# Memory attention beside four projection chunks instead of eight, and four seven-product projection units instead of two

## The reference

```python
h = _rms_norm(x, attn_norm_g[l])
proj = h @ w_in[l]          # 2048 x 13312
da_q, da_k, da_v, r_q, r_k, r_v, r_g, m_q, gates = _split_cols(proj, IN_SIZES)
o_da = _diff_attention(da_q, da_k, da_v, ...)
o_ret = _retention(r_q, r_k, r_v, r_g, ...)
o_mem = _memory_attention(m_q, mem, mem_norm_g[l], w_mem_kv[l], ...)
```

## Time and profile before

| | |
|---|---|
| median of three runs | 1628.24 us |
| profiled execution, first to last instruction | 1625.4 us (2.8 us less than that median; a time of its own for this execution, with launch and end, is not shown) |
| PE busy | 1618.2 us (100%) |
| VectorE busy | 1271.1 us (78%) |
| ScalarE busy | 908.2 us (56%) |
| granted TensorE clock | 1.00 over the whole span |

### The profile page before, as it was taken

How to read it: one execution, slowest core, us unless ns; L and a number is a source line. 1 busy time by engine, 2 the same in 40 slices (tenths; PEclk the granted TensorE clock), 3 DMA queues, 4 the chain that set the end, 5 groups by cost and what they waited for, 6 DMA issues and landing times.

```text
span 1625.4 us, 20227 instructions
## 1 busy us (share of the span) xinstructions
PE 1618.2 (100%) x7373; PEld 1339.3 (82%) x7373; DVE 1271.1 (78%) x1325; ACT 908.2 (56%) x989; POOL 80.6 (5%) x73
## 2 busy tenths in 40 slices
PE   9999999999999999999999999999999999999999
PEld 7888888888888888888888888888888888888887
DVE  5565545589777777777975589999999999999995
ACT  6654454555555554445554465656655665656653
POOL 0000000000011100000000000100100100100101
PEclk9999999999999999999999999999999999999999
DMA  9876555556554555566675756868868868868866
GB/s 339 278 214 194 157 180 175 174 179 220 179 166 162 164 172 168 174 188 199 202 245 182 249 166 207 252 211 248 246 212 250 249 208 249 244 220 240 253 211 178
DMA packets 178007, 341.35 MB, mean 210 GB/s; under 512 B 11793, under 2 KB 16401, under 8 KB 177169
## 3 DMA queue, kind: packets, MB, share of 16 engines
q1 hardware_dynamic: 167056, 319.45, 60.4%
q0 software_dynamic: 10880, 20.97, 7.1%
HBM read 317.31 MB, written 2.10 MB: 197 GB/s over the span
## 4 chain that ended last, share of the span: by engine, by line
PE 90%; issue 6%; DVE 1%; DMA 1%; POOL 1%; ACT 1%; SPq 0%; DVEq 0%; ACTq 0%; POOLq 0%
PE acc L1582 43%; PE at L1664 9%; PE at L1666 9%; PE at L1665 9%; PE acc L1666 5%; PE acc L1664 5%; PE acc L1665 5%; PE at L1582 3%; PE at L1604 2%; POOL rstd L480 1%; PE at L1642 0%; PE at L1657 0%; DMA raw<-in_w_mem_kv 0%; DMA raw<-in_w_in 0%; DVE w_lo L929 0%
## 5 line engine op out<-in xcount | busy, mean ns | idle before, releaser
L929 DVE TENSOR_TENSOR w_lo<-raw,w_hi 128x1024 fp32r<-128x1024 f32 x319 | 386.6, 1222 | 239.6 <-ACT w_hi L507 235.4
L507 ACT ACTIVATE w_hi<-raw 128x1024 fp32r<-128x1024 f32 x319 | 337.1, 1060 | 360.9 <-PE acc L1582 300.3
L1582 PE MATMUL acc<-w_hi,hT_hi 128*128 128x512 f32 x752 | 297.6, 396 | 0.0
L1582 PE MATMUL acc<-w_hi,hT_lo 128*128 128x512 f32 x752 | 293.1, 390 | 0.0
L1582 PE MATMUL acc<-w_lo,hT_hi 128*128 128x512 f32 x752 | 293.0, 390 | 0.0
L857 ACT ACTIVATE f_hi<-sum 128x2048 fp32r<-128x2048 f32 x60 | 115.3, 1922 | 121.2 <-DVE sum L1461 118.0
L1582 PEld LDWEIGHTS acc<-w_hi,hT_hi 128*128 128x128 f32 x752 | 141.2, 188 | 30.9 <-issue 1.3
L1582 PEld LDWEIGHTS acc<-w_hi,hT_lo 128*128 128x128 f32 x752 | 141.2, 188 | 29.7
L1582 PEld LDWEIGHTS acc<-w_lo,hT_hi 128*128 128x128 f32 x752 | 141.3, 188 | 28.4
L1582 PE MATMUL acc<-w_hi,oT_hi 128*128 128x512 f32 x384 | 151.2, 394 | 1.5 <-DVE oT_lo L955 1.4
L1582 PE MATMUL acc<-w_hi,oT_lo 128*128 128x512 f32 x384 | 149.6, 390 | 0.0
(11 more groups left out here) (349 smaller groups left out, 2658.1 us busy)
## 6 DMA issues: line engine op xcount, KB each, us to landing
raw<-in_w_in SPq DMA_DIRECT2D x208, 512.0 KB, 3.8
f_raw<-in_w_ffn_down SPq DMA_DIRECT2D x88, 512.0 KB, 4.8
f_raw<-in_w_ffn_gate SPq DMA_DIRECT2D x80, 512.0 KB, 3.9
f_raw<-in_w_ffn_up SPq DMA_DIRECT2D x80, 512.0 KB, 5.0
proj<-down POOLq DMA_DIRECT2D x40, 512.0 KB, 6.4
raw<-in_w_mem_kv SPq DMA_DIRECT2D x32, 512.0 KB, 6.2
raw<-in_w_out SPq DMA_DIRECT2D x32, 512.0 KB, 3.7
raw<-in_w_o_mem SPq DMA_DIRECT2D x16, 512.0 KB, 5.0
```

The lines of the kernel that those rows point to most:

```text
L507: act.activation(w_hi[:, s % RING], raw[:, s % RING], ACT.Copy).then_inc(hi_done, 1)
L929: v.tensor_tensor(w_lo[:, s % RING], raw[:, s % RING], w_hi[:, s % RING].bitcast(F32), ALU.subtract).then_inc(lo_done, 1)
L1582: e = pe.matmul(dst, a[:, k0 + k, tok], w[:, s % RING, k, :], start=first and k == 0 and n == 0, stop=last and k == 1 and n == 2)
```

## The change

Memory attention is written out over 32 steps (4 plain chunks) instead of 64: a head starts every 7 steps (`HEAD_SLOTS`), at steps 0, 7, 14 and 21, and keeps the offsets of its parts, so that the end of a head (offsets 7 to 11) lies beside the beginning of the next. Its weighted sum goes to another PSUM bank and reads the values where they are, so that a copy of them on ScalarE goes; TensorE's scores wait for the head before to have left that bank. The four plain chunks that are left over go to two more units of seven-product quads: there are now four units (`PJ_UNITS`), the first `nnSnSnSn` as before, the other three `nSnSSnSn` with four `S` quads. Each unit's first `S` quad waits for the direct banks of the unit before (`p_added`). In a unit behind the first, the first `S` quad is the second quad, so VectorE's sums for it stand at step 14 of the unit before, and their low half at step 15, behind `project_added`. `project_scaled` of a unit stands at step 10 of the next.

```diff
-G_PJ = G_PROJ + 64
-PJ_KIND = ("nnSnSnSn", "nnSnSnSn")
-PJ_BLOCKS = (0, 3, 6)
+G_PJ = G_PROJ + 32
+PJ_KIND = ("nnSnSnSn", "nSnSSnSn", "nSnSSnSn", "nSnSSnSn")
+PJ_BLOCKS = tuple("".join(PJ_KIND[:r]).count("S") for r in range(5))
+PJ_UNITS = 4
+HEAD_SLOTS = 7
...
+        def head_slot(x, offset):
+            i, rest = divmod(x - offset, HEAD_SLOTS)
+            return i if rest == 0 and 0 <= i < MEM_H else None
...
# ScalarE (VectorE and TensorE alike: each part of a head under its offset)
-            with act.Fori(0, MEM_H) as i:
-                for s in range(16):
...
-                    if s == 2:
-                        act.activation(v_head, kvm[:, :, ds(i * MEM_D + 1024, MEM_D)],
-                                       ACT.Copy).then_inc(M["values"], 1)
...
+            for x in range(32):
+                memory_attention(x)
+                if x % 8 == 7:
+                    evacuate(G_PROJ + x, x // 8 % 2, 1, proj[:, :, x // 8 * NCOL:(x // 8 + 1) * NCOL])
+                high(G_PROJ + x, x)
+            memory_attention(32)
...
-            for x in range(32):
+            for x in range(16 * PJ_UNITS):
                 j, second = project_pair(x + 4)
...
-                if x == 13:
-                    project_first(0)
-                if x == 26:
-                    project_scaled(0)
-                if x == 29:
-                    project_first(1)
+                if x % 16 == 13:
+                    project_first(x // 16)
+                if x >= 16 and x % 16 == 10:
+                    project_scaled(x // 16 - 1)
...
# VectorE
+                if x % 16 == 13:
+                    project_products(x // 16)
...
+                if x % 16 == 15:
+                    project_added(x // 16)
...
                 if j is not None and not second:
                     project_sums(G_PJ + x, x, j)
                 if second:
                     low_second(G_PJ + x, x)
                     low_project_sums(j)
                 else:
                     low(G_PJ + x, x)
...
# TensorE
+                i = head_slot(x, 5)
+                if i is not None:
+                    pe.wait_ge(M["copied"], i + 1)
+                    if i > 0:
+                        pe.wait_ge(M["lo"], i)
...
-                if first and r == 1:
-                    for p in range(2):
-                        pe.wait_ge(acc_free[p], U_PROJ + 6)
+                if first and r > 0:
+                    pe.wait_ge(p_added, 2 * r)
...
-            for r in range(2):
+            for r in range(PJ_UNITS):
                 for pos in range(8):
                     (project_fast if PJ_KIND[r][pos] == "S" else project_plain)(r, pos)
```

More of the change, by code:

```diff
@@ L227, in program @@
         p_mixed = p_sum[1][:, 1, :].rearrange("p (c m) -> p c m", c=4)
-        p_out = [[proj[:, :, (2 * r + c + 8) * NCOL:(2 * r + c + 9) * NCOL] for c in range(2)] for r in range(2)]
+        p_out = [[proj[:, :, (2 * r + c + 4) * NCOL:(2 * r + c + 5) * NCOL] for c in range(2)] for r in range(PJ_UNITS)]
         gt = proj[:, :, MQ0:MQ0 + NCOL]
@@ L260, in phase_sems @@
             return {n: sem(f"{tag}_{n}") for n in names}
-        M = phase_sems("mem", "squared summed mean root normed values turned copied scored maxed negmax exped recip "
+        M = phase_sems("mem", "squared summed mean root normed turned copied scored maxed negmax exped recip "
                               "weighed pT_ps pT ov hi lo".split())
@@ new lines, in memory_attention @@
+            def memory_attention(x):
+                i = head_slot(x, 11)
+                if i is not None:
+                    act.wait_ge(M["ov"], i + 1)
+                    act.activation(oT_hi[:, 2 * i:2 * i + 2, :], at[:, 2, :].rearrange("p (a b) -> p a b", a=2),
+                                   ACT.Copy).then_inc(M["hi"], 1)
+                i = head_slot(x, 9)
+                if i is not None:
+                    act.wait_ge(M["pT_ps"], i + 1)
+                    act.activation(mem_pT, at[:, 3, :].rearrange("p (a b) -> p a b", a=2),
+                                   ACT.Copy).then_inc(M["pT"], 1)
+                i = head_slot(x, 6)
+                if i is not None:
+                    act.wait_ge(M["negmax"], i + 1)
+                    for t in range(TB):
+                        e = act.activation(pm[:, t, 0:256], at[:, 2, t * 256:(t + 1) * 256], ACT.Exp,
+                                           bias=nmx[:, 0, t:t + 1], scale=MEM_D ** -0.5,
+                                           accum_out=den[:, 0, t:t + 1])
+                    e.then_inc(M["exped"], 1)
+                i = head_slot(x, 5)
+                if i is not None:
+                    act.wait_ge(p_cmb, i * 5 + 5)
+                    act.activation(p_cmb_hi[:, i:i + 1], p_mixed.unsqueeze(1), ACT.Copy).then_inc(p_split, 1)
+                i = head_slot(x, 4)
+                if i is not None:
+                    act.wait_ge(M["turned"], i + 1)
+                    act.activation(qkT, at[:, 0:2, :], ACT.Copy).then_inc(M["copied"], 1)
+                i = head_slot(x, 0)
+                if i is not None:
+                    if i > 0:
+                        act.wait_ge(M["scored"], i)
+                    act.activation(sq[:, :, 0, :], proj[:, :, i * MEM_D + MQ0:(i + 1) * MEM_D + MQ0], ACT.Square)
+                    act.activation(sq[:, :, 1, :], kvm[:, :, i * MEM_D:(i + 1) * MEM_D],
+                                   ACT.Square).then_inc(M["squared"], 1)
@@ L1019, in _ @@
                 low(G_MQ + s, s)
[L1022 to L1055, removed]
-                        v.tensor_tensor(p_mixed[:, 3], a11, a21, ALU.subtract).then_inc(p_cmb, 1)
-                        step(v.tensor_tensor(p_mixed[:, 0], a22, a21, ALU.subtract), p_cmb, i * 5 + 3)
-                        step(v.scalar_tensor_tensor(out=p_mixed[:, 1], in0=p_mixed[:, 0], scalar=-1.0, in1=a11,
-                                                    op0=ALU.mult, op1=ALU.subtract), p_cmb, i * 5 + 4)
-                        v.tensor_tensor(p_mixed[:, 2], a12, p_mixed[:, 1], ALU.add).then_inc(p_cmb, 1)
-                    if s == 8:
-                        v.wait_ge(p_split, i * 2 + 1)
-                        v.tensor_tensor(p_cmb_lo[:, ds(i, 1)], p_mixed.unsqueeze(1),
-                                        p_cmb_hi[:, ds(i, 1)].bitcast(F32), ALU.subtract).then_inc(p_split, 1)
-                    low(i * 16 + (G_PROJ + s), s)
@@ L1067, in diff_means @@
+            for x in range(32):
+                memory_attention(x)
+                low(G_PROJ + x, x)
+            memory_attention(32)
             def diff_means(i):
@@ new lines, in memory_attention @@
+            def memory_attention(x):
+                i = head_slot(x, 10)
+                if i is not None:
+                    pe.wait_ge(M["pT"], i + 1)
+                    for h in range(2):
+                        for k in range(2):
+                            c0 = 1024 + i * MEM_D + h * P
+                            e = pe.matmul(at[:, 2, h * 256:(h + 1) * 256], kvm[:, k, c0:c0 + P], mem_pT[:, k, :],
+                                          start=k == 0, stop=k == 1)
+                    e.then_inc(M["ov"], 1)
+                i = head_slot(x, 8)
+                if i is not None:
+                    pe.wait_ge(M["weighed"], i + 1)
+                    for k in range(2):
+                        for t in range(TB):
+                            e = turn(at[:, 3, k * 256 + t * P:k * 256 + (t + 1) * P], pm[:, t, k * P:(k + 1) * P])
+                    e.then_inc(M["pT_ps"], 1)
+                i = head_slot(x, 5)
+                if i is not None:
+                    pe.wait_ge(M["copied"], i + 1)
+                    if i > 0:
+                        pe.wait_ge(M["lo"], i)
+                    for t in range(TB):
+                        for h in range(2):
+                            e = pe.matmul(at[:, 2, t * 256:(t + 1) * 256],
+                                          qkT[:, 0, h * 256 + t * P:h * 256 + (t + 1) * P],
+                                          qkT[:, 1, h * 256:(h + 1) * 256], start=h == 0, stop=h == 1)
+                    e.then_inc(M["scored"], 1)
+                i = head_slot(x, 3)
+                if i is not None:
+                    pe.wait_ge(M["normed"], i + 1)
+                    for k in range(2):
+                        for h in range(2):
+                            for t in range(TB):
+                                e = turn(at[:, k, h * 256 + t * P:h * 256 + (t + 1) * P],
+                                         qn[:, t, k, h * P:(h + 1) * P])
+                    e.then_inc(M["turned"], 1)
@@ L1662, in product @@
+            for x in range(32):
+                chunk_pair(G_PROJ + x, x, hT_hi, hT_lo, 0, x % 8, 8, U_PROJ + x // 16, x // 8 % 2)
+                memory_attention(x)
             def product(dst, hi, lo, whi, wlo, first, last):
```

184 lines of the change are left out of this document (83 added, 101 removed).

## The result

The changed kernel takes **1630.17 us** (median of 16 runs, 1628.94 to 1631.32); the kernel before takes 1627.31 us (16 runs, 1626.37 to 1628.88). The interval leaves out 1, so the small loss is measured. On the chip of the first four experiments the kernel before took 1626.9 to 1627.7 us in nine runs with a mean granted clock of 1.000 and 1628.3 to 1629.1 in ten with 0.999, so medians of few runs can differ by 1.4 us for that alone. The profiled execution took 1628.94 us with a span of 1627.1, 1.7 more than the span before; it was the shortest of the 16, so that spans show 1.2 us less of the change than medians do.

What follows compares the result with a forecast made beforehand. The prediction took TensorE as the bound, VectorE just behind it. Products -6.12 and stops +8.3 gave +2.1 us, a span of 1627.5; with 2.84 from span to median, 1630.4 us, 8-in-10 range 1625.8 to 1633.4.

Steps and rivals of the forecast that it cites:

- Products, 6.12 us: On TensorE in the units: nine more `S` quads drop 3 products each, 27 x 0.2267 = 6.12 us less.
- Heads, 0: Memory attention's heads in 32 steps: no new gap on TensorE, 0 us taken, bounds 0 and 3 us.
- The rival that priced the heads at 3 us: Two heads beside each other stop TensorE by 1 us in each of the last three: 1633.4 us, chance 0.11.
- From a unit into the next, 3 x 2.52 + 0.70 = 8.3: Three passages between units: TensorE stops for VectorE's queue, 2.52 us each, the first 0.70 more; 8.3 us in all.
- T: The moment when TensorE starts the last plain quad of a unit; VectorE's results were forecast as us behind it.
- The place of the second stop: In the second of two neighbouring `S` quads, units two to four: about 1.4 us lost, ended by the low sums.
- Scaling covered by 1.4 us: ScalarE's scaling near a unit's end: hidden by VectorE's 1.4 us wait for T, costing 0; 0.3 us a unit if uncovered.
- VectorE keeping ahead: Rival for the units: VectorE causes no stops, so all 6.12 us stay gained: 1622.1 us; chance 0.15 with Busy time alone.
- Busy time alone: Rival for the units: occupancy alone decides, 0.3 to 1 us a unit, 1623 to 1625; chance 0.15 with VectorE keeping ahead.
- Loads of the ring: Rival for the last three units: loads freed later land on VectorE's path, over 1631.5 or 1633.4 us; chance 0.12.
- the 0.3 that the prediction named as a sign of being wrong: Sign against the forecast: VectorE's sums ended by a DMA for more than 0.3 us.
- The sum: Whole kernel: -6.12 + 8.3 = +2.1 us on the profiled span, 1625.4 to 1627.5; as median 1630.4 us.

Runs made afterwards that it cites:

- the first four experiments: Four edits of the changed kernel, e1_three_each, e2_first_is_second, e3_neighbours_late and e4_two_more_adds, measured at 1622.53, 1627.63, 1624.09 and 1633.79 us.
- e1_three_each: Changed kernel with three `S` quads in every unit, all four in the first unit's order nnSnSnSn: 1622.53 us, ratio 0.9969 to the kernel before.
- e8_rotation_later: Changed kernel with differential attention's rotation moved from step 11 of the first unit to step 11 of the second: 1629.84 us, one execution.
- e2_first_is_second: Changed kernel with units two to four as nSnSnnSn, three `S` quads each, the first of them second: 1627.63 us, ratio 0.9999 to the kernel before.
- e7_short_products: Changed kernel with the four sums at a unit's end cut to 16 of 512 columns in units one to three: 1627.37 us, ratio 0.9999.
- e4_two_more_adds: Changed kernel with two more unread 128x512 additions on VectorE among the products of units one to three: 1633.79 us, ratio 1.004 to the kernel before.
- e3_neighbours_late: Changed kernel with units two to four as nnSnSSnn, two neighbouring `S` quads, the first one third: 1624.09 us, ratio 0.9973 to the kernel before.

## Why the prediction was right

**Products, 6.12 us.** The heads and the first unit without a gap, and in `e1_three_each` 18 products for 3.96 us of the stage, 4.08 by the rule of 0.2267 a product: confirmed.

**Heads, 0.** From their first product to the first unit's (139.09 to 245.46) 106.4 us for 106.3, and no wait of PE in them. Only the unit's first product is slow, the next one coming 0.42 us later in place of 0.23: 0.2 us. The rival that priced the heads at 3 us has fallen. (The room that the working gave as 2.9 us in the kernel before was 2.6: the first product of that step starts at 151.34, not at 151.59.)

**From a unit into the next, 3 x 2.52 + 0.70 = 8.3.** 8.1 found. The chain of the second passage is as forecast: products at T+0.83 for T+0.83, half low half T+11.89 for T+11.87, the second `S` quad's sums, which need a load, at 341.96, T+16.47 for T+16.47, low sums T+30.29 for T+30.29. (The working goes on with 16.49 for its 16.47; that is 0.02 us.) In the first passage the products began at 283.09, T+1.39 and so 0.56 late, not 0.70. By starts, from T to the next T less 180 products and from the last T to the units' end less 204, the passages cost 3.0, 2.6 and 2.5 us for 3.2, 2.5 and 2.5 forecast.

**The place of the second stop.** About 1.4 us were to be lost inside the second neighbour, ended by the low sums. It is split: a part at that quad's half low half (0.45 idle, 0.61 by starts, in the second passage) and only the rest at the low sums (0.18, 0.34). I followed the low sums alone; the sum was the same, because the last of the two sets it.

**Scaling covered by 1.4 us.** Right in its price, 0, and in the cover, 1.3 us found, but the working did not say how much of it the scaling would use. Ahead of the third unit's products the wait for ScalarE takes 1.11 us, and 0.19 is left before the products could start. `e8_rotation_later` shows what the reserve was then worth: of 1.34 us put into it 1.05 were paid. (The scaling's row says 2.54 us; the 2.45 of the working is the distance to the next start, 402.74 to 405.19.) In the kernel before, VectorE still had 1.65 us to wait at such a place.

**The rivals.** VectorE keeping ahead: 8.1 us of stops say no. Busy time alone: `e1_three_each` and `e2_first_is_second` do the same work, and 5.1 us lie between them. By the rule of the Trainium skill (Perfetto Trace Analysis, section Identifying the Most-Contended Engine), which takes occupancy for VectorE and weight-load time for TensorE, VectorE is the most contended engine there, and the trace agrees, with 93% for weight loads' 100.36 of 130.54 us, 77%. That names the engine; how much is lost depends on the order behind T. Loads of the ring: not in the changed kernel, but close. VectorE's sums waited for one once, 1.08 us at 402.35, which is more than the 0.3 that the prediction named as a sign of being wrong. No stop followed, but narrowly: the low sums that came of it were done at 407.02 + 2.29 = 409.31, and TensorE's first product with them started at 409.38. The loads come next, as `e7_short_products` shows.

**The sum.** Forecast +2.1 on the profiled time; the stage shows +2.12. Spans differ by 1.7, since the beginning ahead of the heads was 0.58 us shorter in the one profile than in the other (139.09 for 139.67), and medians by 2.86; the interval of the ratio, 1.5 to 3.7 us, holds the 2.12. What the 0.7 between the stage and the medians is, no run here tells. That 1630.4 met 1630.17 so closely is luck: the base was a median of three runs, 1628.24, which lies 0.93 above the 1627.31 of sixteen, and the medians moved by 0.8 more than forecast, so two errors cancel. The time in the stage was no luck: its terms were found one by one, to 0.2 us.

Left open: what a version with four quads would take if the loads came earlier as well. It wasn't tried; three quads without any stop keep 4.08 of the 6.12 us, so at most 2.0 us more are there.

## What to carry to other kernels

A shortcut that spares the bounding engine work by giving more to the second-busiest one is to be priced by the second engine's queue, counted in order from the last moment at which it has to wait for the first, and not by its busy share. Put such pieces where that queue has had time to get ahead again: here one plain quad more behind a unit's end, and three pieces in place of four, turned a loss of 2.1 us in these stages into a gain of 4.0. A wait that looks like spare time (1.4 us here) may already be taken by another engine's work in front of it; look at every idle time in that queue, with its releaser, before counting on it.

## What was not expected of the hardware

In `e4_two_more_adds` the first stop was followed by slow products. The timeline of PE there:
```profile
295.91 0.77 PE L1693 MATMUL acc<-w_hi,hT_hi 128*128 128x512 f32 x1 [2.70 <-DVE w_lo L944]
296.48 0.63 PE L1694 MATMUL acc<-w_lo,hT_hi 128*128 128x512 f32 x1
296.90 0.63 PE L1695 MATMUL acc<-w_hi,hT_lo 128*128 128x512 f32 x1
297.33 0.63 PE L1693 MATMUL at<-w_hi,hT_hi 128*128 128x512 f32 x1
```
and the stretch around it, with one around the second stop (2.19 us at 340.72):
```profile
290.00:300.00 10.00, 7.30 (x26) 5.65 (x25) 9.66 (x9) 4.90 (x5) 0.00 (x0) 0.83 0.49 154
335.00:345.00 10.00, 7.81 (x34) 6.02 (x33) 9.90 (x9) 4.87 (x4) 0.00 (x0) 1.00 0.53 157
```
Products stand 0.42 to 0.43 us apart in place of 0.23, eight of them in all, and the granted clock of these 10 us is 0.83: behind the stop of 2.70 us TensorE ran for a while at 1.2 in place of 2.4 GHz, which cost about 1.6 us of products (8 x 0.2). Behind stops of 2.19 and 2.20 us in the same kernel, and of 2.03 in `e8_rotation_later`, products were back at 0.23 and the clock stayed at 1.00. But in `e3_neighbours_late` the eight slow products at the kernel's start stand behind a wait of only 2.08 us, so the length of the stop alone does not decide; what does, no run here shows. In the 1.6 us of `e4_two_more_adds` VectorE caught up, and the stop in the neighbours of that passage was gone: the price appeared in another place than the one where it was expected, and the total came out close, in part by luck. The prediction had no such term; in the profiled execution of the changed kernel, with stops up to 1.56 us and a clock of 1.00 in all its stretches, it was not needed.
